# A fused float32 model of attention, pooling, recurrence and experts: the second mixer's first four gate chunks are split into heads and rests, as all its others are

## The chip, the core and the metric

The kernel runs on one core of a Trainium2 chip. The time is device microseconds of one execution of the whole program; the number given is the median over several executions. TensorE (PE) multiplies matrices, VectorE (DVE) and ScalarE (ACT) work on elements, GpSimd (POOL) issues some small loads, and SyncE (SP) issues the loads of the weights. Each engine runs its own list of instructions in order, and the engines wait for one another by semaphores.

## The reference, cut to what matters

The model is three blocks on a stream x of 256 tokens by 1024 columns, all in float32. The first block has two layers (l = 0, 1); each is a mixer and a dense feed-forward. The change is in the mixer of the second layer:

```python
h = rms_norm(x, norm1_g[l]) * (1.0 + scale1) + shift1
z = h @ w_in[l]
q, k, v = ...                      # columns 0:512, 512:1024, 1024:1536
o = diff_attention(q, k, v, lam)   # softmax of scores, twice, then @ v
y_attn = rms_norm(o) ... @ w_attn_o[l]
u = ga * jax.nn.sigmoid(gb)        # columns 1536:2560
u = causal_depthwise_conv(u, dw_conv_w[l], dw_conv_b[l])   # 31 taps
y_conv = silu(layer_norm(u)) @ w_conv_o[l]
g_attn, g_conv = jnp.split(jax.nn.sigmoid(z[..., G_OFF:]), 2, axis=-1)  # columns 2560:4608
mixed = (g_attn * y_attn + g_conv * y_conv) @ w_out[l]
x = x + (1.0 + gate1) * mixed
```

The gates are the last 2048 columns of z: a product of h (256 by 1024) with 1024 by 2048 weights. The second block has a mixer of a similar kind (its chunks are untouched), the third two recurrent mixers, one dense feed-forward and eight experts.

## The kernel before

Every weight is cut into chunks of 512 KB, and a chunk is 128 partitions by 2048 elements: four row blocks of 128 by 512 columns. A plan (class `Plan`) lists all chunks in the order of the program. SyncE loads them, in that order, into six buffers `raw`.

**Split chunks.** A float32 product is made as three products of a shorter format (fp32r). ScalarE copies a landed chunk into `head` (`make_head`, L693), which keeps the leading part of each number; VectorE subtracts it from `raw` into `rest` (`make_rest`, L1147). There are three buffers of each. The activations are split in the same way, hT into hTh and hTl. For each block TensorE then runs `three` (L2019 to L2021): head by hTh, rest by hTh, head by hTl. A chunk of a linear layer with 256 tokens takes 8 such triples, 24 instructions of 512 columns.

**Unsplit chunks.** `plan_linear(..., unsplit=True)` puts a chunk's number into a set `UNSPLIT`. ScalarE and VectorE skip such a chunk in their `feed`, TensorE multiplies hT by `raw` in full float32 (L2054), and SyncE takes the chunk's raw buffer as free when TensorE has used it, not when its rest is made. A chunk has 8 such products, each of two instructions in the profile, 16 in all. Before the change the chunks of `gates0.0`, `gates0.1`, `gates1.0` and `gates1.1` are unsplit, two chunks each: the first number is the layer, the second the group of 512 gate columns.

**Semaphores.** `chunk_landed` counts the loads, `heads_done` the heads, `rests_done` the rests (all these by VectorE, in order), and `chunk_used` the chunks that TensorE has finished. A head waits until its chunk has landed and until the chunk three before it has been used (the split buffers). A rest waits for its head. A split chunk's first matmul waits for its rest, an unsplit one's for the landing. The load of place n waits until the chunk of place n - 6 is out of its raw buffer.

**What sets the order.** Nothing schedules: each engine's program is written out by hand. On TensorE the second layer's mixer runs ga, gb, q, k, rotate, v, `scores`, gates1.0, gates1.1, `turn_scores`, `apply_scores` (the product with v), gates1.2, `turn_attention`, gates1.3, `turn_channels`, and the output products. A result in the accumulators is evacuated by ScalarE: `gate_job` (L822) takes a gate group through a sigmoid into `gat`.

ScalarE's and VectorE's programs hold calls of `feed(upto)`, which make all heads or rests not made yet, up to a chunk. On ScalarE each `job(name)` begins with a feed up to two chunks behind the named product, so heads run ahead. On VectorE the feeds stand between the other work of the mixer. From the rotation on its program of layer 1 reads:

```python
feed(last_chunk(f"k{l}") + 1 + AHEAD)
rope(l)
...
probs(l, 0)
probs(l, 1)
feed(last_chunk(f"gates{l}.2") + 1)
conv_taps(l, range(16, 22))
head_scale(l)
```

The first of these feeds reaches the second chunk of v, and the next is the one behind `probs`. In between are `add_taps`, `mask_and_max` (twice) and `conv_taps(l, range(11, 16))`. `conv_taps` (L1516) are the multiply-adds of the depthwise convolution, four instructions a tap; when all are done, VectorE's conv_done releases `turn_channels` on TensorE (L2115). `head_norm` on ScalarE (L860 squares, L864 the root) comes behind the product with v, and `head_scale` (L1529, L1531) behind that on VectorE.

Of the kernel before, what the change touches and what calls it, by code (L numbers as in the profile page):

```python
# [29 lines left out]
NT = 512  # L30
# [107 lines left out]
def column_chunks(w, n0, rows=KD, r0=0):  # L138
    t = tiles(w)
    return [halves(t[:, k:k + 4, n0:n0 + NT], NT) for k in range(r0, r0 + rows, 4)]  # L140


def build(nc, a, out):
# [5 lines left out]
    def plan_norm(splits=True):  # L149
        n = n_norm[0]  # L150
        n_norm[0] += 1
        for t in range(T):
            plan.job(f"norm{n}.{t}", "dve", counted=False)
        for t, half in (HALVES_FIRST if n == 0 else TILES_FIRST) if splits else ():
            plan.split(f"norm{n}.{t}{half}")

    def plan_linear(name, w, cols, evac, n0=0, rows=KD, unsplit=False):
        if unsplit:
            plan.unsplit.update(range(len(plan.chunks), len(plan.chunks) + rows // 4))
        for j in range(cols // NT):  # L160
            plan.job(f"{name}.{j}" if cols > NT else name, evac, column_chunks(w, n0 + j * NT, rows))
# [6 lines left out]
    def queue_mods(*slices):  # L168
        for k, j in slices:
            queue.extend((k, j, q) for q in range(4))  # L170

    def plan_mods(count):
        for _ in range(count):
            k, j, q = queue.pop(0)
            plan.mod(k, j, q, halves(tiles(mod_weights(k))[:, 2 * q:2 * q + 2, j * D:(j + 1) * D], D))

    def plan_rotate(k):
        for part in ("rotq", "rotk"):
            plan.job(f"{part}{k}", "dve")

    def plan_scores(k):
        for q in ("score0", "score1a", "score1b"):
            plan.job(f"{q}.{k}", "act")
# [5 lines left out]
    def plan_apply(k):  # L189
        plan_turns(k)  # L190
        plan.job(f"pv{k}", "dve")
# [14 lines left out]
    def plan_ffn(k, gate, up, down, steps):  # L206
        at3[k] = len(plan.chunks)
        counts_at[k] = dict(plan.count)
        for i, src in enumerate(ffn_sources(gate, up, down, steps)):
            s, part = (i - 4) // 3, (i - 4) % 3  # L210
            if i >= 4 and k in MODS_IN_FFN and s < len(MODS_IN_FFN[k]):
                plan_mods(MODS_IN_FFN[k][s][part])
            plan.weight(src)
# [4 lines left out]
    for l in range(2):  # L218
        if l == 0:
            queue_mods((0, 0), (0, 1))  # L220
            plan_mods(8)
            queue_mods((0, 3), (0, 2), (0, 4))
        plan_norm()
        w = a["w_in"][l]
        plan_linear(f"ga{l}", w, 512, "act", 1536)
        plan.job(f"gb{l}", "act")
        plan.jobs[f"gb{l}"] = plan.jobs[f"gb{l}"][:2] + (2,) + plan.jobs[f"gb{l}"][3:]
        for ch, src in enumerate(column_chunks(w, 2048)):
            plan_mods(2 if l == 0 and ch == 1 else 0)
            plan.weight(src)  # L230
        plan_mods(2 if l == 0 else 0)
        plan_linear(f"q{l}", w, 512, "act", 0)
        plan_linear(f"k{l}", w, 512, "act", 512)
        plan_rotate(l)
        plan_linear(f"v{l}", w, 512, "act", 1024)
        plan_scores(l)
        plan_linear(f"gates{l}.0", w, NT, "act", 2560, unsplit=True)
        plan_linear(f"gates{l}.1", w, NT, "act", 2560 + NT, unsplit=True)
        plan_apply(l)
        plan_linear(f"gates{l}.2", w, NT, "act", 2560 + 2 * NT)  # L240
        plan.job(f"oturn{l}", "act")
        plan.split(f"attn{l}.0")
        plan_linear(f"gates{l}.3", w, NT, "act", 2560 + 3 * NT)
        plan.split(f"attn{l}.1")
        plan.job(f"lnturn{l}", "act")
        plan_linear(f"yattn{l}.0", a["w_attn_o"][l], NT, "dve", rows=KW)
        plan.job(f"lnback{l}", "act")
        plan_mods(1 if l == 0 else 0)
        plan_linear(f"yattn{l}.1", a["w_attn_o"][l], NT, "dve", NT, rows=KW)
        plan.split(f"conv{l}")  # L250
        for j in range(2):
            plan_mods(1 if l == 0 else 0)
            plan_linear(f"yconv{l}.{j}", a["w_conv_o"][l], NT, "dve", j * NT, rows=KW)
        plan.job(f"mix{l}.0", "act")
        plan.job(f"mix{l}.1", "act")
        plan.split(f"mix{l}.0")
        plan.split(f"mix{l}.1")
        for j in range(2):
            plan.job(f"wout{l}.{j}", "dve")
            plan.jobs[f"wout{l}.{j}"] = plan.jobs[f"wout{l}.{j}"][:2] + (2,) + plan.jobs[f"wout{l}.{j}"][3:]  # L260
            for ch, src in enumerate(column_chunks(a["w_out"][l], j * NT)):
                plan_mods((2 if (j, ch) == (0, 0) else 1) if l == 0 else 0)
                plan.weight(src)
        plan_norm()
        queue_mods(*(((0, 5), (1, 3), (1, 4), (1, 2), (1, 0), (1, 1)) if l == 0 else ((1, 5), (2, 0), (2, 1), (2, 2))))
        wf = a["w_ffn_in"][l]
        plan_ffn(l, wf[:, 0:F1], wf[:, F1:2 * F1], a["w_ffn_out"][l], F1 // FB)

    plan_norm()
    w = a["w_in_2"][0]  # L270
# [26 lines left out]
    for l in range(2):  # L297
        plan_norm()
        w = a["w_in_3"][l]
# [2246 lines left out]
```

## Time and profile before

| | before |
|---|---|
| median of 3 runs | 2475.67 us (2475.46 to 2476.18) |
| profiled execution | 2475.45 us |
| its span, first to last instruction | 2473.6 us |
| mean granted TensorE clock | 0.984 of full |
| TensorE busy | 2363.7 us, 96% |
| VectorE busy | 1942.6 us, 79% |
| ScalarE busy | 1419.4 us, 57% |

The page of the profile gives busy times, the chain of work that ended last, and the costliest groups of instructions. The timelines give the instructions of an engine in order, equal neighbours merged, with the idle time ahead of them and what released them in brackets. All times within the program are microseconds from the start of the span. The second layer's mixer lies at about 455 to 640 us of it.

### The profile page before, as it was taken

To read this page: it belongs to the slowest core of one execution; us is meant where nothing else is said; L and a number is where in the kernel's file an instruction comes from. 1 tells how busy PE (TensorE), PEld (TensorE's weight loads), DVE (VectorE), ACT (ScalarE), POOL (GpSimd) and SP (SyncE) were. 2 spreads that over 40 slices of the span, in tenths; PEclk is the share of its full clock that TensorE was granted. 3 is DMA by queue.
4 is the path that set the end of the run, shared out by engine and by line. 5 is a ranking of instruction groups with operands and counts; after the bars stand their busy time and mean duration, and the time that the engine had idled before them with its cause. 6 is when DMAs were issued, how large, how long until landed. Compare 5 with 4: busy or idle time off the path is not lost.

```text
span 2473.6 us, 29836 instructions
## 1 busy us (share of the span) xinstructions
PE 2363.7 (96%) x11895; PEld 1979.3 (80%) x11895; DVE 1942.6 (79%) x1866; ACT 1419.4 (57%) x1410; POOL 17.4 (1%) x33
## 2 busy tenths in 40 slices
PE   4988999998999899899999989999999999999998
PEld 4866788867888798798888978888888888888886
DVE  6998878787797656675445769898989898989897
ACT  2654433546443454455334547777777777777776
POOL 0000000000000000000000000000000000000000
PEclk9998999999999999899999999999999999999999
DMA  9556889444598445445555439999999999999996
GB/s 339 189 181 240 304 294 347 158 139 142 188 340 298 148 158 180 133 165 186 188 195 181 155 131 360 360 363 351 358 351 365 352 361 353 360 354 361 348 365 217
DMA packets 434768, 652.93 MB, mean 264 GB/s; under 512 B 20144, under 2 KB 323888, under 8 KB 434624
## 3 DMA queue, kind: packets, MB, share of 16 engines
q1 hardware_dynamic: 432592, 644.63, 75.3%
q0 software_dynamic: 2032, 6.33, 0.8%
q8 instruction: 97, 1.59, 0.3%
q14 instruction: 47, 0.39, 0.0%
HBM read 649.82 MB, written 1.05 MB: 263 GB/s over the span
## 4 chain that ended last, share of the span: by engine, by line
PE 89%; DVE 7%; ACT 2%; issue 1%; DMA 1%; SPq 0%; ACTq 0%; DVEq 0%
PE pair L2019 27%; PE pair L2021 26%; PE pair L2020 26%; PE pair L2054 2%; PE tb L2230 2%; DVE rest L1147 1%; PE pair L2411 1%; DVE aw L1516 1%; PE pair L2142 1%; DMA raw<-in_ada_w 1%; PE tb L2097 1%; DVE gat L1166 1%; DVE hT L1266 1%; ACT aw L722 0%; PE pair L2155 0%
## 5 line engine op out<-in xcount | busy, mean ns | idle before, releaser
L1147 DVE TENSOR_TENSOR rest<-raw,head 128x2048 fp32r<-128x2048 f32 x544 | 1245.0, 2291 | 295.6 <-ACT head L693 279.9
L693 ACT ACTIVATE head<-raw 128x2048 fp32r<-128x2048 f32 x544 | 1039.3, 1912 | 325.1 <-PE pair L2021 294.2
L2019 PE MATMUL pair<-head,hTh 128*128 128x512 f32 x1864 | 744.2, 399 | 6.3 <-issue 3.0
L2021 PE MATMUL pair<-head,hTl 128*128 128x512 f32 x1864 | 728.3, 391 | 0.0
L2020 PE MATMUL pair<-rest,hTh 128*128 128x512 f32 x1864 | 727.3, 390 | 0.0
L2019 PEld LDWEIGHTS pair<-head,hTh 128*128 128x128 f32 x1864 | 350.8, 188 | 79.6 <-issue 9.1
L2021 PEld LDWEIGHTS pair<-head,hTl 128*128 128x128 f32 x1864 | 350.3, 188 | 74.4
L2020 PEld LDWEIGHTS pair<-rest,hTh 128*128 128x128 f32 x1864 | 351.1, 188 | 69.4 <-issue 1.2
L2019 PE MATMUL pair<-head,aTh 128*128 128x512 f32 x776 | 308.4, 397 | 4.0 <-issue 2.9
L2020 PE MATMUL pair<-rest,aTh 128*128 128x512 f32 x776 | 303.7, 391 | 0.0
L2021 PE MATMUL pair<-head,aTl 128*128 128x512 f32 x776 | 303.7, 391 | 0.0
L2019 PE MATMUL pair<-hTh,head 128*128 128x256 f32 x736 | 211.3, 287 | 15.4 <-issue 7.2
L2020 PE MATMUL pair<-hTl,head 128*128 128x256 f32 x736 | 209.9, 285 | 0.0
L2021 PE MATMUL pair<-hTh,rest 128*128 128x256 f32 x736 | 209.8, 285 | 0.0
L928 ACT ACTIVATE aTh<-tb 128x256 fp32r<-128x256 f32 (+1 forms) x145 | 62.8, 433 | 231.3 <-PE tb L2230 231.3
L2019 PEld LDWEIGHTS pair<-head,aTh 128*128 128x128 f32 x776 | 146.6, 189 | 38.5 <-issue 9.1
L2021 PEld LDWEIGHTS pair<-head,aTl 128*128 128x128 f32 x776 | 146.6, 189 | 31.2
L2020 PEld LDWEIGHTS pair<-rest,aTh 128*128 128x128 f32 x776 | 146.8, 189 | 30.5 <-issue 1.0
L924 ACT ACTIVATE qkv<-pair 128x256 f32<-128x256 f32 (+1 forms) x148 | 64.6, 436 | 174.8 <-PE pair L2021 174.8
L2019 PEld LDWEIGHTS pair<-hTh,head 128*128 128x128 f32 x736 | 143.0, 194 | 17.0 <-issue 8.8
L2020 PEld LDWEIGHTS pair<-hTl,head 128*128 128x128 f32 x736 | 143.1, 194 | 0.1
L2021 PEld LDWEIGHTS pair<-hTh,rest 128*128 128x128 f32 x736 | 142.9, 194 | 0.0
(302 smaller groups left out, 1637.8 us busy)
## 6 DMA issues: line engine op xcount, KB each, us to landing
raw<-in_moe_w_gate SPq DMA_DIRECT2D x224, 512.0 KB, 5.2
raw<-in_moe_w_up SPq DMA_DIRECT2D x224, 512.0 KB, 7.2
raw<-in_moe_w_down SPq DMA_DIRECT2D x224, 512.0 KB, 5.6
raw<-in_w_in SPq DMA_DIRECT2D x152, 512.0 KB, 4.6
raw<-in_ada_w SPq DMA_DIRECT2D x96, 512.0 KB, 5.5
raw<-in_w_ffn_in SPq DMA_DIRECT2D x88, 512.0 KB, 5.3
raw<-in_w_ffn_out SPq DMA_DIRECT2D x44, 512.0 KB, 5.4
raw<-in_w_out SPq DMA_DIRECT2D x40, 512.0 KB, 4.3
```

Of the source, the lines that this page charges most:

```text
L693: act.activation(head[:, c.split, :], raw[:, c.raw, :], ACT.Copy).then_inc(heads_done, 1)
L924: act.activation(sg[:, 0:nt, :], src, ACT.Silu).then_inc(sem("silu_ready"), 1)
L928: act.activation(aTh[:, :, 0:nt * P], tb[0][:, :].rearrange("p (k s) -> p k s", k=2)[:, :, 0:nt * P], ACT.Copy).then_inc(ath_ready, 1)
L1147: dve.tensor_tensor(rest[:, c.split, :], raw[:, c.raw, :], head[:, c.split, :].bitcast(F32), ALU.subtract).then_inc(rests_done, 1)
L1166: ins = dve.scalar_tensor_tensor(out=acc, in0=src, scalar=c_, in1=acc, op0=ALU.mult, op1=ALU.add)
L1266: ins = dve.tensor_scalar(hT[:, k, toks], ps[:, i, :], scale[:, k:k + 1], shift[:, k:k + 1], ALU.mult, ALU.add)
L1516: did(dve.scalar_tensor_tensor(out=conv[:, g, :], in0=upad[:, g, k:k + S], scalar=w_, in1=conv[:, g, :], op0=ALU.mult, op1=ALU.add))
L2019: pe.matmul(out_, lh, rh, start=start, stop=False, skip_group_check=True)
L2020: pe.matmul(out_, lh, rl, start=False, stop=False, skip_group_check=True)
L2021: return pe.matmul(out_, ll, rh, start=False, stop=stop, skip_group_check=True)
L2054: ins = pe.matmul(ps[:, t, :], hT[:, kk, toks], raw[:, c.raw, wcols], start=first, stop=last, skip_group_check=True)
L2230: ins = pe.transpose(tb[0][:, k * S + t * P:k * S + (t + 1) * P], act_[:, t, k * P:(k + 1) * P], ident)
```

## The change

Two lines of the plan. In layer 1 `gates1.0` and `gates1.1` are no longer unsplit: their four chunks get heads on ScalarE and rests on VectorE and are multiplied by `three`. In layer 0 nothing changes.

```diff
         plan_linear(f"v{l}", w, 512, "act", 1024)
         plan_scores(l)
-        plan_linear(f"gates{l}.0", w, NT, "act", 2560, unsplit=True)
-        plan_linear(f"gates{l}.1", w, NT, "act", 2560 + NT, unsplit=True)
+        plan_linear(f"gates{l}.0", w, NT, "act", 2560, unsplit=l == 0)
+        plan_linear(f"gates{l}.1", w, NT, "act", 2560 + NT, unsplit=l == 0)
         plan_apply(l)
         plan_linear(f"gates{l}.2", w, NT, "act", 2560 + 2 * NT)
```

The feeds are not edited, but what they make follows from the set `UNSPLIT`. VectorE in layer 1's mixer, at the second `probs` (L1580 and L1584 write the probabilities into xn), then rests, then taps. Before:

```order
L1577 TENSOR_SCALAR sm<-sm 128x4
L1580 TENSOR_SCALAR xn<-xn,sm 128x256 x4
L1584 SCALAR_TENSOR_TENSOR xn<-xn,sm 128x256 x4
L1147 TENSOR_TENSOR rest<-raw,head 128x2048 x2
L1516 SCALAR_TENSOR_TENSOR aw<-upad,prm,aw 128x256 x24
L1529 RECIPROCAL sm<-sm 128x8
```

The same place after the change:

```order
L1577 TENSOR_SCALAR sm<-sm 128x4
L1580 TENSOR_SCALAR xn<-xn,sm 128x256 x4
L1584 SCALAR_TENSOR_TENSOR xn<-xn,sm 128x256 x4
L1147 TENSOR_TENSOR rest<-raw,head 128x2048 x6
L1516 SCALAR_TENSOR_TENSOR aw<-upad,prm,aw 128x256 x24
L1529 RECIPROCAL sm<-sm 128x8
```

Four rests are added, all in the row behind the probabilities.

ScalarE from the evacuation of k (the first L822 into qkv) to the copies of the turned scores (L848); L827 and L833 take the scores, L840 are the exponentials, L822 into gat the gates. Before:

```order
L822 ACTIVATE qkv<-pair 128x1024 x2
L827 ACTIVATE oT<-pair 128x1024
L833 ACTIVATE xn<-pair 128x2x512 x2
L840 ACT_TABLE_LOAD
L840 ACTIVATE oT,sm<-oT,sm 128x128 x8
L840 ACTIVATE xn,sm<-xn,sm 128x256 x8
L822 ACT_TABLE_LOAD
L822 ACTIVATE gat<-pair 128x2x512
L693 ACTIVATE head<-raw 128x2048 x2
L822 ACTIVATE gat<-pair 128x2x512
L848 ACTIVATE aw<-pair 128x1024
```

After:

```order
L822 ACTIVATE qkv<-pair 128x1024
L693 ACTIVATE head<-raw 128x2048 x2
L822 ACTIVATE qkv<-pair 128x1024
L827 ACTIVATE oT<-pair 128x1024
L833 ACTIVATE xn<-pair 128x2x512 x2
L840 ACT_TABLE_LOAD
L840 ACTIVATE oT,sm<-oT,sm 128x128 x8
L840 ACTIVATE xn,sm<-xn,sm 128x256 x8
L693 ACTIVATE head<-raw 128x2048 x2
L822 ACT_TABLE_LOAD
L822 ACTIVATE gat<-pair 128x2x512
L693 ACTIVATE head<-raw 128x2048 x2
```

Two heads come in ahead of the evacuation of v, and two behind the exponentials.

TensorE behind the score products (L2166), with the semaphores that an instruction waits for. Before:

```order
L2166 MATMUL pair<-qkv 128x256 x3
L2054 MATMUL pair<-raw,hT 128x512 [waits chunk_landed5,evac_act]
L2054 MATMUL pair<-raw,hT 128x512 x7
L2054 MATMUL pair<-raw,hT 128x512 [waits chunk_landed0]
L2054 MATMUL pair<-raw,hT 128x512 x7
```

After:

```order
L2166 MATMUL pair<-qkv 128x256 x3
L2019 MATMUL pair<-head,hTh 128x512 [waits rests_done,evac_act]
L2020 MATMUL pair<-rest,hTh 128x512
L2021 MATMUL pair<-head,hTl 128x512
L2019 MATMUL pair<-head,hTh 128x512
L2020 MATMUL pair<-rest,hTh 128x512
```

The first matmul of each gate chunk now waits for a rest, where it waited for a landing. On SyncE the order of the loads is the same; four of them wait for rests_done where they waited for chunk_used.

## Rows read from the trace of the kernel before

**Rows 1.** The page: engines' busy time, the chain by engine, the w_in loads.

```profile
PE 2363.7 (96%) x11895; PEld 1979.3 (80%) x11895; DVE 1942.6 (79%) x1866; ACT 1419.4 (57%) x1410; POOL 17.4 (1%) x33
...
PE 89%; DVE 7%; ACT 2%; issue 1%; DMA 1%; SPq 0%; ACTq 0%; DVEq 0%
...
raw<-in_w_in SPq DMA_DIRECT2D x152, 512.0 KB, 4.6
```

**Rows 2.** TensorE's timeline, 504 to 580 us: start, duration, instruction, [idle before].

```profile
505.04 0.39 PE L2020 MATMUL pair<-rest,hTh 128*128 128x512 f32 x1
...
515.51 0.39 PE L2021 MATMUL pair<-head,hTl 128*128 128x512 f32 x1
515.83 2.89 PE L2166 MATMUL pair<-qkv 64*128 64x128 f32 x32
518.65 27.73 PE L2054 MATMUL pair<-raw,hT 128*128 128x512 f32 x64
546.22 0.60 PE L2178 MATMUL pair<-cst,oT 128*128 128x128 f32 x4
...
577.44 1.94 PE L2115 MATMUL pair<-cst,aw 128*128 128x128 f32 x8 [2.83 <-DVEq L1713]
```

**Rows 3.** VectorE's timeline, 500 to 556 us.

```profile
500.39 2.29 DVE L1147 TENSOR_TENSOR rest<-raw,head 128x2048 fp32r<-128x2048 f32 x1
...
518.09 1.23 DVE L1564 TENSOR_TENSOR oT<-oT,cst 128x1024 f32<-128x1024 f32 x1 [4.66 <-ACT oT L827]
...
537.13 1.67 DVE L1584 SCALAR_TENSOR_TENSOR xn<-xn,sm 128x256 f32<-128x256 f32 x4
538.95 2.29 DVE L1147 TENSOR_TENSOR rest<-raw,head 128x2048 fp32r<-128x2048 f32 x1
541.56 2.29 DVE L1147 TENSOR_TENSOR rest<-raw,head 128x2048 fp32r<-128x2048 f32 x1 [0.31 <-ACT head L693]
543.77 10.21 DVE L1516 SCALAR_TENSOR_TENSOR aw<-upad,prm,aw 128x256 f32<-128x256 f32 x24
555.77 0.20 DVE L1529 RECIPROCAL sm<-sm 128x8 f32<-128x8 f32 x1 [1.79 <-ACT sm L864]
```

**Rows 4.** ScalarE's timeline, 501 to 560 us.

```profile
515.93 1.02 ACT L822 ACTIVATE qkv<-pair 128x1024 f32<-128x1024 f32 x1 [13.36 <-PE pair L2021]
...
528.53 1.28 ACT L822 ACT_TABLE_LOAD   x1
...
539.61 1.91 ACT L693 ACTIVATE head<-raw 128x2048 fp32r<-128x2048 f32 x1 [4.10 <-PE pair L2054]
546.42 1.03 ACT L822 ACTIVATE gat<-pair 128x1024 f32<-128x1024 f32 x1 [4.90 <-PE pair L2054]
...
555.64 3.76 ACT L693 ACTIVATE head<-raw 128x2048 fp32r<-128x2048 f32 x2
```

**Rows 5.** The chain that ended last, 550 to 585 us: start, length, whose.

```profile
551.95 2.17 ACT oT L860 x16
...
555.43 0.31 ACT sm L864
...
581.15 0.43 PE pair L2020
```

**Rows 6.** TensorE after two waits; then stretch: us, PE busy (x), PEclk, DMA share, GB/s.

```profile
46.69 0.58 PE L2019 MATMUL pair<-hTh,head 128*128 128x256 f32 x1 [6.61 <-DVE hTl L1275]
...
1037.73 0.55 PE L2019 MATMUL pair<-hTh,head 128*128 128x256 f32 x1 [1.43 <-issue]
...
46.70:51.40 4.70, 4.70 (x22) 0.50 0.80 310
51.70:60.00 8.30, 8.30 (x72) 1.00 0.59 203
...
1037.70:1041.20 3.50, 3.47 (x16) 0.50 0.36 140
```

**Rows 7.** One of TensorE's waits: us in total, times, longest.

```profile
PE pair L2132 <- DVE gat L1601: 13.0, 4, 5.6
```

## Prediction

> **What bounds the kernel now.** The page comes first. TensorE is busy 96% of the span and holds 89% of the chain of work that ended last, VectorE only 7% [rows 1]. That average says that TensorE's instructions are the time, and it is the wrong guide for this edit: the change touches one place of some 28 us, so that place is read alone, in the timelines of TensorE, VectorE and ScalarE from 501 to 585 us, and then in the chain there.
>
> I call the second mixer's gate chunks g0 to g7 (gates1.0 has g0, g1; gates1.1 g2, g3; gates1.2 g4, g5; gates1.3 g6, g7). TensorE's timeline [rows 2]: the v projection ends, the score products (L2166) follow at 515.83, and at 518.65 the 64 unsplit instructions of g0 to g3 (L2054) start without a wait. They run until 546.22, where the turning of the scores (L2178) starts. Those instructions read raw, so all they need is a landed chunk.
>
> VectorE in the same stretch [rows 3]: after the last rest (500.39, of the v projection's second chunk) it ropes, masks, makes taps and probabilities until 538.8, and only then its next two rests, at 538.95 and 541.56: those of g4 and g5. Then 24 taps from 543.77. The reader is to see that no rest is made between 500.39 and 538.95.
>
> From 546.22 to 577 the chain leaves TensorE [rows 4, 5]: evacuation of gates1.1 at 546.42, two copies, the product with v, the squares of head_norm from 551.95, the root at 555.43, VectorE's reciprocal at 555.77, then taps and rests on VectorE in one unbroken row, the last of which releases TensorE's turn_channels at 577.44 [rows 2]. So whatever moves 546.22 moves 577.44, unless VectorE's taps become later than the root. TensorE stood idle for 2.83 us before 577.44; it has nothing to give back there.
>
> **What the change removes and adds.** TensorE: 64 instructions of L2054 go, 27.57 us from 518.65 to 546.22. In their place come 4 x 24 = 96 instructions of L2019 to L2021. Their pace is read on the v projection: from the start at 505.04 to that at 515.51 there are 46 steps, 0.2276 us each [rows 2]. 96 x 0.2276 = 21.85 us, so TensorE has 5.7 us less to do. The Trainium skill (FP8 and Floating Point Precision, TensorE Precision Notes) says that a true fp32 product takes four passes through the array, while the split one takes three; by that rule the edit shortens the kernel. By that rule, the rows agree on the work: 27.57 against 21.85 us. They don't agree on the time, since the rule knows no wait.
>
> ScalarE: four more heads of 1.9 us (as at 539.61, [rows 4]). Those of g0 and g1 now stand ahead of the evacuation of v, where ScalarE idles 13.36 us until 515.93 [rows 4]; their buffers are free when the last chunk of k and the first of v have been used, at 501.4 and (24 steps behind 505) about 510.4, so they end near 512.4 and cost nothing. Without that cover they would push the scores by 3.8 us. That of g2 stands behind the exponentials, near 528.5, also idle time. That of g3 needs the buffer of g0 and so waits for TensorE.
>
> VectorE: four more rests of 2.29 us. They are not put where they are needed. feed() makes rests in the order of the chunks, and the first feed that reaches a gate chunk is the one behind the probabilities, where two rests turn into six. That is the step that decides.
>
> SyncE: the loads into the buffers of g0 to g3 now wait for rests instead of for TensorE. g6's load goes from g0's use (518.65 and a quarter of 27.57 us, about 525.5) to g0's rest (541.2), and lands in about 4.6 us (the median of these loads, [rows 1]); its head is wanted at 555.64 now and later still after the change. The four loads move to 541, 543.5, 546 and some 554, still ahead of their readers. Nothing.
>
> **The wait that comes in.** TensorE now waits at g0 for its rest. VectorE's path to there is untouched, so that rest starts at 538.95 and ends at 541.24, and TensorE starts at about 541.3 instead of at 518.65: 22.65 us idle. Behind the waiting matmul stand, on TensorE's queue, all four gate chunks, the turning of the scores and the product with v; for that product waits head_norm, and for that VectorE.
>
> From there TensorE is the slowest of the three. The rests of g1 and g2 end at 543.5 and 545.8, long before they are wanted. g3's head waits for g0 used, then 1.91 + 2.29 = 4.2 us; it is wanted 10.9 us after g0 is used. So TensorE runs through: 541.3 + 21.85 = 563.15 at the full clock.
>
> The clock does not stay full. After 6.61 us idle TensorE ran 256-column products from 46.69, 22 in 4.70 us, and 72 in 8.30 us from 51.7; the granted clock was 0.50 in the first stretch and 1.00 in the second [rows 6]. Those are the levels of 1.2 and 2.4 GHz. The 512-column step at the low level is 0.43 us [rows 5]. In 4.8 us at that level pass the first instruction (0.55 us) and ten at 0.43; at the full level these 11 take 2.5 us, so the loss is 2.3 us. Bounds: a shorter dense run at the low level behind a wait is 3.5 us (1037.7 to 1041.2, [rows 6]), a loss of 1.7; if the low level lasted until g0 is through, 24 steps lose 24 x 0.2 = 4.8. Behind the wait of 2.83 us at 577.44 the steps are slow as well [rows 5]. I take 2.3, since 46.69 is the one dense start that directly follows a long idle stretch.
>
> **The sum.** TensorE reaches the turning of the scores at 541.3 + 21.85 + 2.3 = 565.45 instead of 546.22: 19.2 us late. The root and the reciprocal come 9.55 us behind, at 575.0. VectorE meanwhile: g5's head waits for g2 used (about 560.0), its rest ends some 4.2 us behind, at 564.3, and the 24 taps (10.2 us) end at 574.5, just ahead of the reciprocal. So here TensorE's path still decides, by half a microsecond, and all that follows to 577.44 and beyond shifts by 19.2 us. The page's own execution: 2475.45 (span 2473.6) + 19.2 = 2494.65. The median of the runs is 0.22 above that execution: 2475.67 + 19.2 = 2494.9 us. Range of this case: loss of clock 1.7 to 4.8, 18.6 to 21.7 us, 2494.3 to 2497.4; with a microsecond each way for how the later low stretches fall, 2493.3 to 2498.4.
>
> **Rivals.**
> A. The clock is back at once. Then the shift is 16.9 us (563.15 - 546.22), 2492.6. For it: only that the low stretch was short in places. Against: rows 6.
> B. Lockstep: head, rest and matmul of g3, g5 and the next ones follow one another with no overlap, since there are three split buffers. Price 4.2 us for each chunk so held, one to two of them: 2499 to 2503. It decides where head plus rest take more than the two chunks in between (10.9 us); they take 4.2, so it needs ScalarE or VectorE to be held by something else at that moment.
> C. Part is given back later, where later work has slack. TensorE waits 13.0 us for L1601 in this trace [rows 7], but that is on work that shifts too. Price: 2480.6 to 2491.
> D. Not slower: the rests stand when TensorE comes. This is the rule of the passes, as a mechanism of this kernel. It decides at 518.65: if g0's rest ends by then, TensorE has no wait and ends 5.7 us earlier. VectorE has 4.66 us idle before 518.09 [rows 3] and 1.79 before 555.77, against 4 x 2.29 = 9.2 us of new work, so the result lies between -5.7 (2470.0) and +2.7 us (2478.4). Against it: the order has all four behind the probabilities, 22.6 us too late.
>
> **How the numbers follow.** My forecast 78%; A 8%; B 5%; C 6%; D 3%. Time 2494.9. The range takes the main case and A, and leaves most of B, C and D: 2491.5 to 2499.5. About 0.2% (5 us) is what a measurement of this kernel can tell from no change, so below 2470.7 is faster and above 2480.6 slower: faster 1%, same 2%, slower 97%.
>
> **What would show it.** TensorE idle for 22 to 23 us with a rest as its releaser, in place of none at 518.65; VectorE's six rests from 538.95, the fourth waiting for a head near 551 to 552, the sixth ending near 564; TensorE's 0.43 us steps for 4 to 5 us behind 541.3; the turning of the scores near 565.4 and turn_channels near 596.7. The forecast is wrong if a rest of a gate chunk stands ahead of the probabilities, if the first mixer moves at all (its rows should repeat), or if the shift at turn_channels isn't that at the end.

## The result, and the profile after

| | before | changed |
|---|---|---|
| median (4 runs each, the same chip) | 2475.77 us | 2497.26 us (2495.92 to 2497.65) |
| profiled execution | 2475.45 us | 2497.65 us |
| its span | 2473.6 us | 2495.8 us |

The ratio is 1.0082, with a 95% interval of 1.0070 to 1.0094: the change costs 21.5 us (0.9%). The forecast was 2494.9 us in a range of 2491.5 to 2499.5.

The page of the changed kernel, engines' busy time and then the chain by engine (it answers to [rows 1]):

```profile
PE 2362.4 (95%) x11927; PEld 1989.0 (80%) x11927; DVE 1951.7 (78%) x1870; ACT 1427.4 (57%) x1414; POOL 17.4 (1%) x33
...
PE 88%; DVE 7%; ACT 2%; issue 1%; DMA 1%; SPq 0%; DVEq 0%; ACTq 0%
```

TensorE is busy 1.3 us less than before although the program is 22 us longer. The page shows no more than that; the place shows the rest. TensorE's timeline of the changed kernel (start, duration, instruction, idle before and releaser), from g0 to turn_channels; it answers to [rows 2]:

```profile
541.00 0.77 PE L2019 MATMUL pair<-head,hTh 128*128 128x512 f32 x1 [22.67 <-DVE rest L1147]
541.56 0.63 PE L2020 MATMUL pair<-rest,hTh 128*128 128x512 f32 x1
...
546.20 0.39 PE L2019 MATMUL pair<-head,hTh 128*128 128x512 f32 x1
...
565.24 0.60 PE L2178 MATMUL pair<-cst,oT 128*128 128x128 f32 x4
...
596.47 1.14 PE L2115 MATMUL pair<-cst,aw 128*128 128x128 f32 x8 [2.82 <-DVEq L1713]
```

This execution began 0.4 us earlier than the one before (the v projection's products start at 504.65 instead of 505.04). So L2178 comes 565.24 - 546.22 + 0.39 = 19.4 us late by the program's own time, and turn_channels 596.47 - 577.44 + 0.39 = 19.4 us too. The idle time ahead of turn_channels is what it was, 2.82 us.

VectorE in the same stretch (as [rows 3]):

```profile
536.74 1.67 DVE L1584 SCALAR_TENSOR_TENSOR xn<-xn,sm 128x256 f32<-128x256 f32 x4
538.56 6.70 DVE L1147 TENSOR_TENSOR rest<-raw,head 128x2048 fp32r<-128x2048 f32 x3
551.13 2.29 DVE L1147 TENSOR_TENSOR rest<-raw,head 128x2048 fp32r<-128x2048 f32 x1 [5.88 <-ACT head L693]
557.42 2.29 DVE L1147 TENSOR_TENSOR rest<-raw,head 128x2048 fp32r<-128x2048 f32 x1 [4.00 <-ACT head L693]
562.01 2.29 DVE L1147 TENSOR_TENSOR rest<-raw,head 128x2048 fp32r<-128x2048 f32 x1 [2.29 <-ACT head L693]
564.22 10.21 DVE L1516 SCALAR_TENSOR_TENSOR aw<-upad,prm,aw 128x256 f32<-128x256 f32 x24
574.79 0.20 DVE L1529 RECIPROCAL sm<-sm 128x8 f32<-128x8 f32 x1 [0.37 <-ACT sm L864]
```

The first three rests run together behind the probabilities. The next three wait for heads. Each of these heads waits until TensorE has used an earlier chunk: g3's and g5's for the split buffer itself, and g4's because it stands on ScalarE behind the evacuation of gates1.0 (554.56), which waits for g1's products. The taps end 0.37 us ahead of the root. ScalarE (as [rows 4]):

```profile
510.17 1.92 ACT L693 ACTIVATE head<-raw 128x2048 fp32r<-128x2048 f32 x1 [6.17 <-PE pair L2021]
515.54 1.02 ACT L822 ACTIVATE qkv<-pair 128x1024 f32<-128x1024 f32 x1 [3.46 <-PE pair L2021]
...
549.18 1.92 ACT L693 ACTIVATE head<-raw 128x2048 fp32r<-128x2048 f32 x1 [19.26 <-PE pair L2021]
```

g1's head ends at 512.1, before v is to be evacuated, and costs nothing. g3's head waits 19.26 us for g0 to be used.

The granted clock, in stretches from to, TensorE's busy time (instructions), PEclk, DMA share, GB/s:

```profile
518.26:541.00 22.74, 0.07 (x3) 0.59 0.00 0
541.00:546.00 5.00, 5.00 (x12) 0.50 0.77 258
546.00:565.30 19.30, 19.30 (x87) 1.00 0.58 206
```

It fell within the wait and stayed at the lower of its two levels (1.2 GHz) for 5 us of dense products, then rose to 2.4 GHz.

### The profile page after: what moved, and what is told of

The parts are those of the page before. It is cut to its first block, busy times and chain, and to the rows that moved or that the text cites. A ratio compares the mean times of both kernels' runs of the same rounds, so it can differ in the third digit from the quotient of the medians.

```text
span 2495.8 us, 29912 instructions
## 1 busy us (share of the span) xinstructions
PE 2362.4 (95%) x11927; PEld 1989.0 (80%) x11927; DVE 1951.7 (78%) x1870; ACT 1427.4 (57%) x1414; POOL 17.4 (1%) x33
## 4 chain that ended last, share of the span: by engine, by line
PE 88%; DVE 7%; ACT 2%; issue 1%; DMA 1%; SPq 0%; DVEq 0%; ACTq 0%
PE pair L2019 27%; PE pair L2021 27%; PE pair L2020 27%; PE tb L2230 2%; DVE aw L1516 1%; DVE rest L1147 1%; PE pair L2411 1%; PE pair L2054 1%; PE pair L2142 1%; DMA raw<-in_ada_w 1%; PE tb L2097 1%; DVE gat L1166 1%; ACT aw L722 0%; PE pair L2155 0%; DVE hT L1266 0%
## 5 line engine op out<-in xcount | busy, mean ns | idle before, releaser
L2019 PE MATMUL pair<-head,hTh 128*128 128x512 f32 x1896 | 758.5, 400 | 28.6 <-DVE rest L1147 24.8
L2021 PE MATMUL pair<-head,hTl 128*128 128x512 f32 x1896 | 742.1, 391 | 0.0
L2020 PE MATMUL pair<-rest,hTh 128*128 128x512 f32 x1896 | 741.3, 391 | 0.0
L2019 PEld LDWEIGHTS pair<-head,hTh 128*128 128x128 f32 x1896 | 357.9, 189 | 103.9 <-issue 31.8
L2021 PEld LDWEIGHTS pair<-head,hTl 128*128 128x128 f32 x1896 | 357.2, 188 | 76.0
L2020 PEld LDWEIGHTS pair<-rest,hTh 128*128 128x128 f32 x1896 | 358.2, 189 | 71.1 <-issue 1.2
L2019 PE MATMUL pair<-head,aTh 128*128 128x512 f32 x776 | 308.6, 398 | 4.8 <-issue 3.7
L2021 PE MATMUL pair<-head,aTl 128*128 128x512 f32 x776 | 304.0, 392 | 0.0
L2019 PE MATMUL pair<-hTh,head 128*128 128x256 f32 x736 | 211.9, 288 | 15.6 <-issue 8.0
L2021 PE MATMUL pair<-hTh,rest 128*128 128x256 f32 x736 | 210.6, 286 | 0.0
L2019 PEld LDWEIGHTS pair<-head,aTh 128*128 128x128 f32 x776 | 146.7, 189 | 39.2 <-issue 9.8
L2021 PEld LDWEIGHTS pair<-head,aTl 128*128 128x128 f32 x776 | 146.8, 189 | 31.2
L2019 PEld LDWEIGHTS pair<-hTh,head 128*128 128x128 f32 x736 | 143.8, 195 | 16.9 <-issue 8.8
L2021 PEld LDWEIGHTS pair<-hTh,rest 128*128 128x128 f32 x736 | 143.8, 195 | 0.0
```

Source lines behind the costliest of these rows:

```text
L2019: pe.matmul(out_, lh, rh, start=start, stop=False, skip_group_check=True)
L2020: pe.matmul(out_, lh, rl, start=False, stop=False, skip_group_check=True)
L2021: return pe.matmul(out_, ll, rh, start=False, stop=stop, skip_group_check=True)
```

## Experiments

Each kernel was timed on one chip beside the kernel before, whose medians there were 2475.03 us (e1 to e4), 2476.57 us (e5 to e8) and 2475.81 us (e10, e11), with single executions from 2473.55 to 2479.43; ratios are against those. The expectations give times from the medians on record before, 2475.67 and 2475.77; where the chip's own median differs, the cost is what is to be compared. "Shift" is the start of an instruction on TensorE less that of the same instruction in the trace of before, less the shift that stood at 208 us already, since an execution can begin up to 2 us early or late. For e8, e10 and e11, which are edited ahead of 208 us as well, shifts are given as they stand.

### Which half of the change costs (e1, e2)

In the first, g0 and g1 alone are split in layer 1:

```diff
-plan_linear(f"gates{l}.1", w, NT, "act", 2560 + NT, unsplit=l == 0)
+plan_linear(f"gates{l}.1", w, NT, "act", 2560 + NT, unsplit=True)
```

> Half of the change: in layer 1 only g0 and g1 are split, g2 and g3 stay unsplit. Theory W (the wait for g0's rest is the price, the products themselves are cheaper): TensorE starts at 541.0 as in the changed kernel, 10.9 us of products plus 2.4 us of low clock, then 13.85 us of unsplit products, so the turning of the scores comes at 568.2, 22.3 us late. Half of the change then costs MORE than all of it: 2498 to 2501. Rival N (each newly split chunk costs its head and rest, so the cost goes by their number): half of 21.5, about 2486.5.

In the second, g2 and g3 alone:

```diff
-plan_linear(f"gates{l}.0", w, NT, "act", 2560, unsplit=l == 0)
+plan_linear(f"gates{l}.0", w, NT, "act", 2560, unsplit=True)
```

> The other half: g0 and g1 stay unsplit, g2 and g3 are split. Theory W: TensorE has 13.85 us of work before it asks for a rest (532.1), the rest of g2 is there at 540.8, so it waits 8.7 us, then 10.9 us of products and about 2.2 us of low clock: turning of the scores at 554, 8.2 us late, VectorE's taps ending at 562.7 just ahead of the root at 563.5. 2484 to 2486. Rival N: half of 21.5, about 2486.5, as in the other half.

Measured: 2498.4 us for the first pair (ratio 1.0093, 1.0076 to 1.0110) and 2484.18 us for the second (1.0035, 1.0022 to 1.0047). TensorE's timeline with the first pair split:

```profile
539.09 0.76 PE L2019 MATMUL pair<-head,hTh 128*128 128x512 f32 x1 [22.66 <-DVE rest L1147]
...
552.31 13.89 PE L2054 MATMUL pair<-raw,hT 128*128 128x512 f32 x32
566.04 0.60 PE L2178 MATMUL pair<-cst,oT 128*128 128x128 f32 x4
```

and with the second pair split:

```profile
541.23 0.77 PE L2019 MATMUL pair<-head,hTh 128*128 128x512 f32 x1 [8.72 <-DVE rest L1147]
...
554.58 0.60 PE L2178 MATMUL pair<-cst,oT 128*128 128x128 f32 x4
```

The same number of heads and rests, and a cost of 23.4 against 9.2 us. What decides is how long the first split chunk waits: 22.66 us where it is g0, 8.72 where it is g2, since TensorE then has 13.85 us of unsplit products to do first. From g0's start to L2178 the half change needs 566.04 - 539.09 = 26.95 us, the whole one 565.24 - 541.00 = 24.24: once the wait is paid, two more split chunks make it 2.7 us shorter. Whether the half as a whole is slower than the whole can't be said from the totals, whose intervals overlap; the traces say it of this place. That a cost goes by the number of chunks is refuted.

### The place of two rests (e3)

```diff
                 add_taps(l, (3, 4))
+                if l == 1:
+                    feed(last_chunk("gates1.0") + 1)
                 mask_and_max(l, 0)
```

> The changed kernel with one feed more on VectorE, which makes the rests of g0 and g1 ahead of the first mask, where it idled 4.66 us. Nothing else. Theory W (it is the place of the rests in VectorE's order): TensorE starts g0 at 518.3 without a wait, ends g1 at 529.2, waits for g2's rest until about 541 and reaches the turning of the scores near 554, 8 us later than the kernel before: 2484 to 2486. If the price were the rests' work itself (VectorE 9.2 us more), moving two of them changes nothing: 2497.

Measured: 2483.5 us (1.0036, 1.0021 to 1.0050). The two rests in VectorE's timeline, and TensorE's wait that is left; the numbers of lines behind the added ones are two higher here:

```profile
512.25 4.49 DVE L1147 TENSOR_TENSOR rest<-raw,head 128x2048 fp32r<-128x2048 f32 x2
517.00 1.23 DVE L1564 TENSOR_TENSOR oT<-oT,cst 128x1024 f32<-128x1024 f32 x1 [0.26 <-ACT oT L827]
```

```profile
540.28 0.77 PE L2021 MATMUL pair<-head,hTh 128*128 128x512 f32 x1 [11.52 <-DVE rest L1147]
...
553.71 0.60 PE L2180 MATMUL pair<-cst,oT 128*128 128x128 f32 x4
```

VectorE's 4.66 us of idle time take both, and 13 of the 21.5 us are gone (8.5 are left). No instruction was taken out; one call of feed in VectorE's list does it. So the order is the cause of these 13 us, not the work. It isn't the cause of all: the work's part is measured in e6 and e7.

### The clock term (e4)

```diff
                 scores(l)
+                if l == 1:
+                    for i in range(94):
+                        pe.matmul(tb[0][:, :], hTh[:, i % 8, 0:P], hTl[:, 0:2, :]..., start=True, stop=True)
                 linear(f"gates{l}.0", NT)
```

> The changed kernel with 94 products of 512 columns (hTl by hTh into an accumulator that nothing reads there) on TensorE ahead of g0, which fill 21.4 of the 22.7 us of its wait. They add nothing to the output. Theory of the clock term: the granted clock stays 1.00, g0 to g3 take 21.9 instead of 24.3 us, the turning of the scores comes 2.3 us earlier than in the changed kernel and the time is 2494 to 2495.5. If the slow start were something else than the idle stretch (the first use of the buffers, say), g0 still takes 2.4 us more and the time stays 2497.

Measured: 2491.85 us (1.0067, 1.0050 to 1.0084). The clock through the filled wait and the gates:

```profile
518.00:540.08 22.08, 20.98 (x93) 1.00 0.00 0
540.08:561.93 21.85, 21.85 (x96) 1.00 0.71 241
```

The 96 products take 21.85 us, to the digit the figure of 96 x 0.2276 in the forecast, against 24.24 in the changed kernel. So the clock term is 2.4 us (2.3 forecast), shown by taking it away. The shift at L2178 is 17.1 us instead of 19.4. But the median lies below the 2494 to 2495.5 expected. Against the changed kernel the time fell by 3.7 us by the ratios (1.0067 against 1.0082) and by 5.4 by the medians (2491.85 against 2497.26, timed apart), instead of 2.3. The intervals of the two ratios overlap, so the times alone don't show that it fell by more. The trace says where more could come from: the shift stays within 0.3 us from 546 to the end, while that of the changed kernel grows behind the mixer. That is the next question.

### A delay without a split (e5)

The kernel before, with 84 such products ahead of g0 in layer 1:

```diff
                 scores(l)
+                if l == 1:
+                    for i in range(84):
+                        pe.matmul(tb[0][:, :], hTh[:, i % 8, 0:P], hTl[:, 0:2, :]..., start=True, stop=True)
```

> The kernel before (unsplit) with 84 products of 512 columns on TensorE ahead of g0 in layer 1, which nothing reads: 19.1 us of pure delay, TensorE busy all the while, no split, no wait. It tells how a delay at this place reaches the end. The turning of the scores comes 19.1 us late. Theory P (a shift of this size makes later low-clock stretches fall differently on the program): the end moves by 19 to 22 us, and the difference arises at the norms near 1021 and at the router near 1461 us. Rival (the 2 us that the changed kernel lost behind the mixer are a consequence of the split itself, by loads or buffers): the end moves by 19.1 us and nothing is added behind.

Measured: 2494.73 us (1.0071, 1.0056 to 1.0087), 18.2 us above the median beside it. In the profiled execution, the slowest of the four, the shift is 19.4 at L2178 and 21.0 at the end; 1.0 of the growth comes between 834 and 868 us of the trace of before, at the norm behind the second dense feed-forward, 0.4 behind 1021, 0.2 at the router. So in this trace a delay with nothing split grows too, but at other places than expected, and the medians show no growth. The clock there, and then at the same norm in the kernel before:

```profile
853.90:867.50 13.60, 10.51 (x49) 0.50 0.00 0
...
833.40:843.60 10.20, 7.51 (x32) 0.51 0.00 0
```

The low stretch is 3.4 us longer with the delay, and its end falls on the first products behind the norm, which take 0.41 us each there and 0.28 in the kernel before.

### VectorE's part alone (e6)

```diff
                 probs(l, 1)
+                for _ in range(4 if l == 1 else 0):
+                    did(dve.tensor_reduce(sm[:, 144:146], x[:, :, :], AX.X, ALU.max))
+                    now()
                 feed(last_chunk(f"gates{l}.2") + 1)
```

> The kernel before with four reductions of x (2048 elements, 2.29 us each as in its trace) on VectorE behind the probabilities of layer 1, where the change puts four rests. TensorE's and ScalarE's work is untouched; nobody waits for the result. It measures VectorE's part alone. By the rows of before, 1.79 + 0.31 us idle stand ahead of the reciprocal, so head_scale and all behind it move by 9.2 - 1.8 = 7.4 us: 2482 to 2483.5. If TensorE's list were what bounds this place, VectorE's work would hide: 2475 to 2476.

Measured: 2484.22 us (1.0031, 1.0020 to 1.0042); 7.7 us. VectorE's timeline:

```profile
538.36 9.25 DVE L1704 TENSOR_REDUCE sm<-x 128x2 f32<-128x2048 f32 x4
547.64 4.50 DVE L1147 TENSOR_TENSOR rest<-raw,head 128x2048 fp32r<-128x2048 f32 x2
552.06 10.22 DVE L1516 SCALAR_TENSOR_TENSOR aw<-upad,prm,aw 128x256 f32<-128x256 f32 x24
562.19 0.20 DVE L1529 RECIPROCAL sm<-sm 128x8 f32<-128x8 f32 x1
```

The reciprocal comes at 562.19 instead of 555.77, with no idle time before it, and the shift at turn_channels is 7.3 us. So 9.2 us of work that nobody reads, on an engine with 7% of the chain, cost 7 to 8 us here. In its trace, one of the slower executions (2486.21 us), the shift grows on from 7.3 to 10.9 us at the end, again with nothing split.

### All rests where they are needed (e7)

```diff
+                if l == 1:
+                    feed(last_chunk("gates1.0") + 1)
                 mask_and_max(l, 0)
                 mask_and_max(l, 1)
-                conv_taps(l, range(11, 16))
+                if l == 1:
+                    feed(last_chunk("gates1.1"))
+                conv_taps(l, range(11, 15))
+                if l == 1:
+                    feed(last_chunk("gates1.1") + 1)
+                conv_taps(l, range(15, 16))
```

and on ScalarE, ahead of the exponentials of layer 1, `feed(last_chunk("gates1.1"))`.

> The changed kernel (all four split) with every rest where TensorE needs it: g0 and g1 in VectorE's idle time before the first mask, g2 behind the second mask, g3 between two taps, and g2's head on ScalarE ahead of the exponentials. TensorE then waits under 1 us in the gates and ends them at 541, 5 us earlier than the kernel before; but VectorE has 9.2 us more and finds only 6.8 us idle. Theory (VectorE bounds this place once TensorE's wait is gone): conv_done comes 2.4 us later than before, 2477 to 2479. If TensorE's 5.7 us saved count, 2470 to 2471.

Measured: 2478.77 us (1.0006, 0.9997 to 1.0015). TensorE's timeline, with its line numbers moved by the edits (L2028 is L2019, L2187 is L2178):

```profile
518.96 0.50 PE L2028 MATMUL pair<-head,hTh 128*128 128x512 f32 x1
...
535.90 0.50 PE L2028 MATMUL pair<-head,hTh 128*128 128x512 f32 x1 [0.29 <-DVE rest L1149]
541.48 0.60 PE L2187 MATMUL pair<-cst,oT 128*128 128x128 f32 x4
```

L2178 comes 5.2 us earlier than in the kernel before, nearly all that TensorE saves. Then TensorE waits for VectorE: 1.44 us within the turning of the scores, 4.42 at the first chunk of gates1.3 and 0.93 ahead of turn_channels. So turn_channels comes 1.9 us later (2.4 expected). The 5.7 us of TensorE are worth nothing at this place. By the interval the kernel can't be told from the one before. Placing the rests (and g2's head) where they are needed thus takes about 19 of the 21.5 us back; the 2 or so that are left are VectorE's added work.

### A tap moved (e8)

```diff
-                conv_taps(l, range(16, 22))
+                conv_taps(l, range(16, 23))
                 head_scale(l)
-                conv_taps(l, range(22, 24))
+                conv_taps(l, range(23, 24))
```

> The kernel before with one tap of the convolution (four instructions, 1.7 us) moved on VectorE from behind head_scale to ahead of it, in both mixers. It fills VectorE's idle time there, 0.96 us in layer 0 and 1.79 us in layer 1. If VectorE's unbroken row is what sets turn_channels, both mixers end that much earlier, 2.7 us together: ratio 0.9989, about 2472.5. If the time in front of head_scale were of no account, no change.

Measured: 2475.95 us (0.9994, 0.9985 to 1.0003): no difference that can be told, and the expected 0.9989 isn't excluded either. The place itself did as expected. turn_channels in the two mixers:

```profile
172.28 1.07 PE L2115 MATMUL pair<-cst,aw 128*128 128x128 f32 x8 [1.80 <-DVEq L1713]
...
575.48 1.06 PE L2115 MATMUL pair<-cst,aw 128*128 128x128 f32 x8 [1.13 <-DVEq L1713]
```

Against [rows 2] the second is 1.96 us earlier, and TensorE's wait there is 1.7 us shorter. In this execution it is then lost: at 834 us of the trace of before the shift is -0.4, after a low-clock stretch at 608 us that the trace of before doesn't have, and behind 1021 it is +0.7, where low-clock stretches fall on other work. The expectation took a gain at the place for a gain at the end; whether some of it is left over many executions stays open.

### TensorE kept busy in its gaps (e10 in the kernel before, e11 in the changed one)

```diff
             def turn_channels(l):
+                pe.wait_ge(hth_ready, plan.splits[f"attn{l}.0"])
+                keep_busy(11)
                 free(f"lnturn{l}")
...
                 free(f"norm{n}.{t}")
+                keep_busy({(4, 0): 14, (4, 1): 3, (5, 0): 13, (5, 1): 20}.get((n, t), 0))
                 pe.wait_ge(sem("diag_ready"), 2 * n + t + 1)
```

where `keep_busy(count)` makes products of aTh by itself into tb[1].

> The kernel before (unsplit) with products of 512 columns that nothing reads in TensorE's idle time: 11 ahead of turn_channels in both mixers of the first block, 14 and 3 ahead of the two turned norms behind the second dense feed-forward, 13 and 20 ahead of those behind the second block. They are sized to the gaps (2.8, 3.6, 0.95, 3.3 and 5.0 us). Theory: the low-clock stretches behind these gaps go, and with them the slow turning products (3.75 instead of 2.02 us for 16) that stand on the path: 2 to 6 us faster than the kernel before, 2470.5 to 2474.5. Rival: the low clock costs nothing there, as other engines set those places: 2476.

> The same added products in the changed kernel (split). It is to be read against the one before it. Theory P (what the changed kernel lost behind the mixer is how the low-clock stretches fall on the norms and the router): with the stretches at the norms gone in both, the difference between these two is the wait's 19.4 us plus at most the router's 2 us, that is 19.4 to 21.4, and at the norms near 1021 us the shift is unchanged. Rival (the loss at 1021 us comes from the split): the shift still grows by 1.4 us there.

Measured: 2471.01 us in the kernel before (0.9981, 0.9972 to 0.9990) and 2489.17 us in the changed one (1.0054, 1.0040 to 1.0067). The first is faster than both kernels of this case. Its norms behind the second block (L2112 are the added products, L2150 is L2142):

```profile
1018.73 3.11 PE L2112 MATMUL tb<-aTh 128*128 128x512 f32 x13
1022.07 2.05 PE L2150 MATMUL pair<-diag,xn 128*128 128x128 f32 x16 [0.24 <-DVE diag L1254]
...
1026.70 4.70 PE L2112 MATMUL tb<-aTh 128*128 128x512 f32 x20
1031.76 2.05 PE L2150 MATMUL pair<-diag,xn 128*128 128x128 f32 x16 [0.36 <-DVE diag L1254]
```

The same 32 turning products in the kernel before:

```profile
1021.35 3.44 PE L2142 MATMUL pair<-diag,xn 128*128 128x128 f32 x16 [3.27 <-DVE diag L1254]
...
1032.54 3.76 PE L2142 MATMUL pair<-diag,xn 128*128 128x128 f32 x16 [4.99 <-DVE diag L1254]
```

Each 16 take 1.4 to 1.7 us less at the full clock, and from 1021 to 1074 us of the trace of before the shift falls by 4.1 us. (Just ahead of that, at the output product of the second block, this execution lost 1.4 us by a low stretch that the one before doesn't have.)

Between the two kernels lie 18.2 us, below the 19.4 to 21.4 expected, instead of the 21.5 of the pair without these products. Single executions spread over 5.1 and 2.8 us, so the 1.2 us that are missing aren't clear of noise. Between their traces the shift is 18.66 us at 868 and 18.71 at 2456, where it grew by 2.6 us in the pair without: nothing is added behind the mixer, neither near 1021 nor at the router. The start of the second block's output product, which had the low clock in the changed kernel and the full one in the kernel before, has the low clock in both here, first unsplit, then split:

```profile
998.10:1001.10 3.00, 2.95 (x7) 0.50 0.00 0
...
1016.80:1019.70 2.90, 2.90 (x7) 0.50 0.03 6
```

So it doesn't take the split to put a low stretch there, and the rival, a late cost of the split itself, is gone. Between 585 and 830 us the difference fell by 1.6 us in these two traces, since the kernel before had a low-clock stretch there at 608 us and the changed one none on the same work; in the traces, that is what lies below the expected range.

## Why the prediction was right, point by point

- **The step that decides**, that all new rests come behind the probabilities and TensorE waits for the first: 22.67 us idle measured, 22.65 worked out, with the rest as releaser. e1 to e3 show it as the cause: the wait shrinks to 8.72 and 11.52 us, and the cost with it.
- **TensorE's products**: 96 x 0.2276 = 21.85 us; measured without the clock's part 21.85 (e4). That is 0.79 of the 27.57 us before. The three against four of the prediction's rule, where the three is this kernel's own count (L2019 to L2021), would be 0.75: right in its direction, and of no use for the time.
- **The clock**: 2.3 taken, 2.4 measured, low for about 5 us from 541.0. Shown by e4. Rival A, a clock that is back at once, is out.
- **Heads**: those of g0 and g1 end at 512.1 (about 512.4 worked out) and delay nothing; that of g3 starts at 549.18.
- **Loads**: SyncE issues the first of the four that were put off, g6's, at 540.88 us (541 in the forecast), and g6's head waits for nothing but its turn behind the root. They cost nothing, as forecast.
- **VectorE a half microsecond ahead of the root**: 0.37 us. The tally that TensorE's path still decides held by that little.
- **Shift at the place**: 19.4 us measured, 19.2 worked out, the same at L2178 and at turn_channels. But the prediction called itself wrong "if the shift at turn_channels isn't that at the end", and it isn't: 19.4 us there, 21.5 between the medians. That sign came up, and it points at the last term below.
- **Rival B** (lockstep) did not occur: TensorE runs through g0 to g3. **Rival C** (given back later) neither. **Rival D** (not slower): e7 makes its case by moving the rests, and even then the kernel isn't faster; its bounds of -5.7 to +2.7 us hold the measured 1.9 at turn_channels near their upper end.
- **The term that was too small** is "a microsecond each way for how the later low stretches fall". In the profiled execution the shift grows by 2.4 us behind 546: 1.4 us at the output product of the second block, and 1.2 at the router, less 0.2 by small changes of both signs elsewhere. The measured 2497.26 still lies within the 2494.3 to 2497.4 that the prediction gave for this case without that term. That is luck: this room was made for a clock loss of up to 4.8 us, which was 2.4, and something else filled it.

The router in the changed kernel, its clock by stretch and then its products (L2387, 8 columns each):

```profile
1481.70:1485.50 3.80, 3.80 (x21) 0.50 0.00 0
...
1482.20 4.27 PE L2387 MATMUL tb<-trig,hT 128*128 128x8 f32 x20
```

In the kernel before:

```profile
1461.30:1464.70 3.40, 2.61 (x25) 0.99 0.00 0
...
1461.61 2.30 PE L2387 MATMUL tb<-trig,hT 128*128 128x8 f32 x20
```

The same 20 products, 4.27 against 2.30 us. The clock fell ahead of them in one and behind them in the other, though the engine did the same in both. Of the 2.4 us that the shift grows here 1.2 come back at the gather products behind, which had the low clock in the kernel before. The other place is the start of the output product of block two:

```profile
1017.60:1020.80 3.20, 3.16 (x8) 0.53 0.00 0
```

against the kernel before, where the same stretch of the program had the full clock:

```profile
998.74:1001.94 3.20, 3.16 (x14) 1.00 0.00 0
```

8 products where 14 passed. The executions of the changed kernel, 2495.92 to 2497.65, span 1.7 us, so this term is partly drawn anew in each. What draws it isn't settled: the runs show that it moves when the program is delayed (e5, e8), that nothing is left of it between e10 and e11, whose low stretches from 868 us on stand on the same work, and not which delay is a lucky one. That it makes up the 2.3 us between 19.2 and 21.5 is seen in the profiled executions, which are the fastest of before and the slowest of the changed kernel, and not measured over many.

## What to carry to other kernels

A flag that turns a fused operation into a prepared one adds the preparation wherever the helper engine's list next asks for it, so look up that place before counting what the main engine saves: here 5.7 us saved were bought with 22.7 us of waiting, and one call of feed added at the right place takes 13 of the 21.5 us back. Read the bound at the place, not on the page: VectorE held 7% of the chain and still 7 to 8 of the 9.2 us added to it came through. Work that nobody reads, in an idle TensorE that is about to be needed, can pay: it took 4.8 us off the kernel before.

## What the runs showed of the hardware that was not expected

The position of the low-clock stretches is worth as much as a small edit. A gain of 1.7 us at its place (e8) was gone at the end of its trace, and a loss of 19.4 us came out as 21.5. A stretch that starts a few microseconds earlier, with the engine doing the same work, nearly doubled the time of the router's small products (2.30 to 4.27 us). And one and the same gap can be followed by either level: the eight products of turn_channels took 1.94 us behind 2.83 us of idle time in the kernel before [rows 2] and 1.14 us behind 2.82 us in the changed one. The clock fell in both, just ahead of the products in the one and 0.9 us after the first of them in the other, when all eight had started. The changed kernel, first up to the fall and then behind it:

```profile
596.40:597.30 0.90, 0.83 (x8) 1.00 0.00 0
597.40:604.00 6.60, 4.80 (x13) 0.50 0.54 185
```
